# Constant products in TensorE's waits, the last two squares singly, and stages that begin with high-part products

## The reference, cut to what matters

```python
def reference(x, c, ...):                      # x: (1, 256, 1024)
    cond = jax.nn.silu(c)
    for i in range(4):
        mod = (cond @ ada_w[i] + ada_b[i])[:, None, :]
        sh1, sc1, gt1, sh2, sc2, gt2 = jnp.split(mod, 6, axis=-1)
        h = rms_norm(x, norm1_w[i]) * (1 + sc1) + sh1
        y = mixer_of_layer_i(h)                # Mamba-2, RWKV-7, attention, Mamba-2
        x = x + (1 + gt1) * y
        h = rms_norm(x, norm2_w[i]) * (1 + sc2) + sh2
        x = x + (1 + gt2) * swiglu_ffn(h, ffn_w1[i], ffn_w3[i], ffn_w2[i])
    return x

def rms_norm(x, w, eps=1e-6):
    return x * lax.rsqrt(jnp.mean(x * x, axis=-1, keepdims=True) + eps) * w

def swiglu_ffn(h, w1, w3, w2):                 # 1024 -> 2816 -> 1024
    return (jax.nn.silu(h @ w1) * (h @ w3)) @ w2
```

## Time and profile before

| | us |
|---|---|
| median of 3 runs | 1813.46 (1809.7 to 1821.83) |
| the profiled execution | 1818.18 |
| its span, first to last instruction | 1816.1 |
| PE busy | 1697.3 |
| DVE busy | 1314.9 |
| ACT busy | 886.5 |

### The profile page before, as it was taken

The page is one execution under the profiler, slowest core; times in us unless marked ns, Lnnn a source line. Parts: engine busy times, 40 slices in busy tenths (PEclk is TensorE's granted clock), DMA queues, the critical chain, the costliest instruction groups (busy, mean ns, idle before and its releaser), DMA issues.

```text
span 1816.1 us, 37554 instructions
## 1 busy us (share of the span) xinstructions
PE 1697.3 (93%) x15995; PEld 1592.3 (88%) x15995; DVE 1314.9 (72%) x1890; ACT 886.5 (49%) x1242; POOL 20.5 (1%) x62
## 2 busy tenths in 40 slices
PE   4999889999989987799999998899999999999998
PEld 4998788999967876589999887899999998989998
DVE  7897896899573866568996447588967977857553
ACT  3665754544324141344444556444545758645442
POOL 4000000000000000000000000000000000000000
PEclk9999999999989999899999999899999999999999
DMA  9563565999714400049998351399973532448652
GB/s 337 152 194 126 171 217 167 334 351 351 251 47 139 131 4 4 3 141 325 346 340 286 93 162 48 101 324 333 356 282 116 186 117 71 172 143 287 187 187 70
DMA packets 217799, 347.39 MB, mean 191 GB/s; under 512 B 8416, under 2 KB 175024, under 8 KB 217632
## 3 DMA queue, kind: packets, MB, share of 16 engines
q1 hardware_dynamic: 215856, 344.22, 56.1%
q10 hardware_dynamic: 1648, 0.43, 0.1%
q0 software_dynamic: 128, 0.33, 0.1%
HBM read 343.91 MB, written 1.05 MB: 190 GB/s over the span
## 4 chain that ended last, share of the span: by engine, by line
PE 77%; DVE 9%; DMA 5%; ACT 5%; issue 4%; ACTq 0%; DVEq 0%
PE psum_dve L442 27%; PE psum_act L442 26%; PE psum_acc L442 22%; DMA ring<-in_ffn_w_dram 4%; DVE w_lo L1261 2%; DVE arena L1232 2%; ACT w_hi L1782 1%; PE psum_act L445 1%; PE psum_dve L445 1%; DMA arena<-in_ada_b_dram 1%; DVE arena L1400 0%; DVE arena L1438 0%; DVE x L1356 0%; DVE arena L1457 0%; DVE hT L1334 0%
## 5 line engine op out<-in xcount | busy, mean ns | idle before, releaser
L1261 DVE TENSOR_TENSOR w_lo<-ring,w_hi 128x1024 fp32r<-128x1024 f32 x432 | 518.8, 1222 | 193.0 <-ACT w_hi L1782 190.2
L1782 ACT ACTIVATE w_hi<-ring 128x1024 fp32r<-128x1024 f32 x432 | 458.3, 1061 | 395.9 <-DMA ring<-in_ffn_w_dram 232.8
L442 PE MATMUL psum_dve<-h_lo,w_hi 128*128 128x256 f32 x1216 | 341.6, 281 | 0.0
L442 PE MATMUL psum_act<-h_lo,w_hi 128*128 128x256 f32 x960 | 273.1, 284 | 0.0
L1232 DVE SCALAR_TENSOR_TENSOR arena<-ring,vcol,arena 128x512 f32<-128x512 f32 x336 | 239.0, 748 | 5.0 <-DMA ring<-in_ada_w_dram 1.5
L442 PEld LDWEIGHTS psum_dve<-h_lo,w_hi 128*128 128x128 f32 x1216 | 230.0, 189 | 0.0
L442 PE MATMUL psum_act<-h_hi_ffn,w_hi 128*128 128x256 f32 x704 | 201.7, 287 | 11.1 <-DVE h_lo L1331 11.1
L442 PE MATMUL psum_acc<-g_hi,w_hi 128*128 128x256 f32 x704 | 201.1, 286 | 0.0
L442 PE MATMUL psum_act<-h_hi_ffn,w_lo 128*128 128x256 f32 x704 | 201.0, 286 | 0.0
L442 PE MATMUL psum_dve<-h_hi_ffn,w_hi 128*128 128x256 f32 x704 | 197.3, 280 | 0.2 <-DVE w_lo L1261 0.2
L442 PE MATMUL psum_acc<-g_hi,w_lo 128*128 128x256 f32 x704 | 197.4, 280 | 0.0
(11 more groups left out here) (314 smaller groups left out, 3338.6 us busy)
## 6 DMA issues: line engine op xcount, KB each, us to landing
ring<-in_ffn_w_dram SPq DMA_DIRECT2D x132, 1024.0 KB, 7.1
ring<-in_ada_w_dram SPq DMA_DIRECT2D x96, 1024.0 KB, 7.0
ring<-in_m_in_w_dram SPq DMA_DIRECT2D x48, 1024.0 KB, 5.4
ring<-in_m_out_w_dram SPq DMA_DIRECT2D x16, 1024.0 KB, 4.8
ring<-in_r_w_rkv_dram SPq DMA_DIRECT2D x12, 1024.0 KB, 5.4
ring<-in_f_qkvf_w_dram SPq DMA_DIRECT2D x12, 1024.0 KB, 5.3
ring<-in_r_out_w_dram SPq DMA_DIRECT2D x4, 1024.0 KB, 4.8
ring<-in_f_out_w_dram SPq DMA_DIRECT2D x4, 1024.0 KB, 4.8
```

The lines of the kernel that those rows point to most:

```text
L442: return nc.tensor.matmul(o, l, r, start=start, stop=stop, skip_group_check=True)
L1261: tell(V.tensor_tensor(o, raw, hi, ALU.subtract), split_ready, hold=False)
L1782: tell(A(o, raw, ACT.Copy), hi_ready)
```

## The change

- `keep_busy(n)` is new: n plain f32 products of the identity with a constant mask, into `psum_acc[0]`. 20 stand at the start, behind the masks and before the wait for the vectors; 3 before and 4 behind `reduce_part(0, 1)`; one before the last pair of sums of each later norm; behind the sums (and `reduce_part`, where it is) 5 in second norms, 8 in layer 1's first norm, 2 in the first norms of layers 2 and 3.
- The last two tiles are squared singly; a new semaphore tells that the seventh tile is updated.
- `first_tiles` makes the high-part products of all eight tiles first, waiting for `h_hi` alone, and the low-part ones behind them. In a network a third unit's high-part products stand between; its low-part ones and the fourth unit follow.
- DVE scales all eight tiles before the first low part.
- At the start one unit is split before the second modulation part and one behind it, not three before both; the first modulation part is read earlier; ACT splits the two units behind Ln and Exp.

```diff
-FIRST_UNITS = 3
...
+        cond_ready, seventh_ready = sem("cond_ready"), sem("seventh_tile_updated")
...
+            def keep_busy(n):
+                for _ in range(n):
+                    mm(psum_acc[0][:, 0:S], ident[:, :], upto[:, 0:S])
             def freed(key, who):
...
-            def first_tiles(who, narrow=False):
+            def h_high(k):
+                need = KD * (count["split norms"] - 1) + k + 1
+                pe.wait_ge(h_hi_ready, need)
+                return h_hi2[count["which"]][:, k, :]
+            def first_tiles(who, narrow=False, more=None):
+                bn = None
                 if narrow and who == "act":
...
                 else:
-                    bn = open_bank("act") if narrow else None
-                    b = open_bank(who)
+                    if narrow:
+                        bn = open_bank("act")
+                    b, b2 = open_bank(who), open_bank(more) if more else None
                 w = [[v.rearrange("p (k c) -> p k c", k=KD) for v in next_unit()] for u in range(2)]
                 for k in range(KD):
-                    h = h_parts(k)
+                    h = h_high(k)
                     if narrow:
-                        last = mm3(bn[0:M_H, 0:S], (wn_hi[:, k, :], wn_lo[:, k, :]), h, k == 0, k == KD - 1)
+                        mm(bn[0:M_H, 0:S], wn_hi[:, k, :], h, k == 0, False)
+                        mm(bn[0:M_H, 0:S], wn_lo[:, k, :], h, False, False)
+                    for u in range(2):
+                        o = b[:, u * S:(u + 1) * S]
+                        mm(o, w[u][0][:, k, :], h, k == 0 and u == 0, False)
+                        mm(o, w[u][1][:, k, :], h, False, False)
+                if more:
+                    w.append([v.rearrange("p (k c) -> p k c", k=KD) for v in next_unit()])
+                    for k in range(KD):
+                        mm(b2[:, 0:S], w[2][0][:, k, :], h_high(k), k == 0, False)
+                        mm(b2[:, 0:S], w[2][1][:, k, :], h_high(k), False, False)
+                for k in range(KD):
+                    low = h_parts(k)[1]
+                    if narrow:
+                        last = mm(bn[0:M_H, 0:S], wn_hi[:, k, :], low, False, k == KD - 1)
                         if k == KD - 1:
...
                     for u in range(2):
-                        last = mm3(b[:, u * S:(u + 1) * S], (w[u][0][:, k, :], w[u][1][:, k, :]), h, k == 0 and u == 0, k == KD - 1)
+                        last = mm(b[:, u * S:(u + 1) * S], w[u][0][:, k, :], low, False, k == KD - 1)
                         if k == KD - 1 and u == 0:
...
                 bank_read(who)
+                if more:
+                    for k in range(KD):
+                        last = mm(b2[:, 0:S], w[2][0][:, k, :], h_parts(k)[1], False, k == KD - 1)
+                    unit_read(last)
+                    w = [v.rearrange("p (k c) -> p k c", k=KD) for v in next_unit()]
+                    for k in range(KD):
+                        last = mm3(b2[:, S:2 * S], (w[0][:, k, :], w[1][:, k, :]), h_parts(k), k == 0, k == KD - 1)
+                    close_bank(more, last)
+                    bank_read(more)
...
                         bank.append(open_bank("act"))
-                    pe.wait_ge(nsq_ready, 4 * norms[0] + j + 1)
+                    if j == 3 and count["down"]:
+                        pe.wait_ge(acc_free, 4 * count["down"] - 3)
+                        keep_busy(1)
                     for k in (2 * j, 2 * j + 1):
+                        pe.wait_ge(nsq_ready, 5 * norms[0] + (j + 1 if j < 3 else k - 2))
                         last = mm(bank[0][:, 0:S], ones[:, :], nsq[:, k, :], k == 0, k == KD - 1)
...
                         reduce_part(l, 2)
+                    if count["down"]:
+                        keep_busy(5 if which else 8 if l == 1 else 2)
                     norms[0] += 1
...
                 for i in range(KF // 2):
-                    two_tiles("act") if i else first_tiles("act")
-                    two_tiles("dve")
+                    if i == 0:
+                        first_tiles("act", more="dve")
+                    else:
+                        two_tiles("act")
+                        two_tiles("dve")
                 reduced = dict(ffn_reduced(l))
...
             close_bank("act", tr(b[:, 0:KD], vrow[0:KD, 0, :], KD))
+            pe.wait_ge(masks_ready, 1)
+            keep_busy(20)
             pe.wait_ge(vec_landed, 16 * n_vec_dmas)
...
                 first_norm(j)
+            keep_busy(3)
             reduce_part(0, 1)
+            keep_busy(4)
             for l in range(DEPTH):
...
                                                 op0=ALU.mult, op1=ALU.mult), t_ready, hold=False)
-                    if splits and k:
-                        low(k - 1)
                 if splits:
-                    low(KD - 1)
+                    for k in range(KD):
+                        low(k)
                     split_norms[0] += 1
...
                         tell(V.scalar_tensor_tensor(out=x[:, k, :], in0=psum_acc[j][:, u * S:(u + 1) * S], scalar=gate[:, g, k:k + 1],
-                                                    in1=x[:, k, :], op0=ALU.mult, op1=ALU.add), acc_free if u else dve_step, hold=False)
+                                                    in1=x[:, k, :], op0=ALU.mult, op1=ALU.add),
+                             acc_free if u else seventh_ready if j == 3 else dve_step, hold=False)
                 res[0] += 1
...
                     split_narrow(1, M_H)
-            stream(FIRST_UNITS)
-            dve.wait_ge(vcol_ready, 1)
-            reduced_part(0, 0, False)
+                if i == 6:
+                    dve.wait_ge(vcol_ready, 1)
+                    reduced_part(0, 0, False)
+            stream(1)
             reduced_part(0, 1, False)
+            stream(2)
             for l in range(DEPTH):
...
             def norm(l, which):
-                for j in range(4):
+                for j in range(3):
                     if norms[0]:
...
                     tell(A(flat(nsq[:, 2 * j:2 * j + 2, :]), flat(x[:, 2 * j:2 * j + 2, :]), ACT.Square), nsq_ready, hold=False)
-                if (l, which) == (0, 0):
-                    stream(FIRST_UNITS)
+                if norms[0]:
+                    act.wait_ge(seventh_ready, norms[0])
+                tell(A(nsq[:, 6, :], x[:, 6, :], ACT.Square), nsq_ready, hold=False)
+                if norms[0]:
+                    act.wait_ge(acc_free, 4 * norms[0])
+                tell(A(nsq[:, 7, :], x[:, 7, :], ACT.Square), nsq_ready, hold=False)
                 b = take()
...
                 tell(A(rstd[:, :], rstd[:, :], ACT.Exp, scale=-0.5), rstd_ready)
+                if (l, which) == (0, 0):
+                    stream(2)
                 act.wait_ge(mod_ready[which], l + 1)
```

More of the change, by code:

```diff
@@ L239, in trunk @@
         c_landed, qkw_landed, d_landed, dskip_ready = sem("c_landed"), sem("qk_norm_landed"), sem("d_skip_landed"), sem("d_skip_ready")
-        cond_ready = sem("cond_ready")
+        cond_ready, seventh_ready = sem("cond_ready"), sem("seventh_tile_updated")
         mod_ready = [sem(f"mod_ready{i}") for i in range(2)]
```

## The result

Measured side by side, the changed kernel takes 1791.53 us (median of 4, 1784.56 to 1794.24) against 1813.05 us (median of 4, 1809.7 to 1821.83): ratio 0.9872, interval 0.985 to 0.9894. Three more comparisons gave 0.9873, 0.9849 and 0.9882. The gain is 21.5 us, 13.5 were forecast, and the time lies 1 us outside the range.

The account below looks back on a forecast made before the run. PE was taken as the bound, busy 1697.3 of 1816.1 us, leaving 119 us idle and half-clock time to win. Start, norm gains and cap summed to 13.5 us: 1813.46 - 13.5 = 1800, range 1792.5 to 1807.

Parts of the forecast that it names:

- the forecast's own part of it: Whole kernel: the forecast's own range, 1796 to 1806.7 us, given a chance of 0.63.
- Second norms: Second norms of layers 0 to 3: earlier start plus held clock gain 2.0, 3.2, 2.9, 2.0 us before the weights' cap.
- the cap: Networks of layers 1 and 2: PE runs into its weights, limiting second-norm gains from 3.2 to 2.1 and 2.9 to 1.4.
- the earlier start, 0.5: Second norms: after five constants the first real product starts at 308.43, not 308.96, 0.5 us sooner.
- First norms: First norms of layers 1, 2, 3: constants around reduce_part gain 2.4, 1.2, 1.2 us through earlier start and held clock.
- the high bound of 1.75: First norms of layers 2 and 3: upper end of each gain, taken as 1.2 between 0.25 and 1.75 us.
- Start, 1.2: Kernel start: 20 constants and those around reduce_part gain 1.2 us, between 0.3 (clock half through transposes) and 4.3.
- the fall that I feared: Start: the constants' clock is gone before the ones sums, start worth 0.3, total 12.6; one chance in two.
- Layer 2's lead of 0.15 us: Layer 2's network: low half ends at 1259.40, PE uses it at 1259.54; with 1.25 us from earlier transfers, caps gain at 1.4.
- Constants do not hold the clock: Rival, chance 0.12: clock falls as before, only earlier starts remain, 2.8 us gained, 1811 us.
- constants in the way: Rival, chance 0.05: constants at half clock, 0.82 us each, delay each stage's first product; slower, 1826 us.
- No cap, no fall: Rival, chance 0.20: warm start, clock holds through reduce_part, earlier transfers feed layers 1 and 2 in full; about 1793 us.

Follow-up runs that it names:

- the changed one moved back: Changed kernel, its 20 start constants made 42 products of 120 columns, 128 records in all, so the solve lies as in the kernel before: 1795.65 us, ratio 0.9901.
- the kernel before moved: Kernel before plus 42 one-column products in PE's first long wait, moving later work by 84 records: 1807.96 us, ratio 0.9973.
- the order alone: Changed kernel with keep_busy looping no times, so no constants; squares, product order and start order stay: 1808.09 us, ratio 0.9981 to the kernel before.
- the lean start: Changed kernel without the 20 constants at the start and the 3 ahead of reduce_part: 1793.63 us, ratio 0.9888 to the kernel before.
- the tuned kernel: Changed kernel with 14 start constants, modulation parts later in the ring, 2 constants each in head loop and normalisation: 1784.26 us, ratio 0.983 to the kernel before.

## Why the prediction fell short, point by point

**The step that failed** is the sum's silent one: it has terms for eight norms, and takes each stage between them as it was. In its place the runs showed this: every edit that adds instructions to PE moves all later work against the blocks of its code, and in this kernel one stage feels that, by waits for blocks and by the half clock that comes with them. It is 10.2 us in the profiles shown, 6 to 10 over the profiles at the two places (158.8 and 162.1 in the kernel before, 158.8 in the changed one moved back; 151.6 to 152.3 in four profiles of the change, 152.5 in the kernel before moved). Without the solve's 10.2 us the profiled pair differs by 15.0, which is inside the range. Moved back, the change measures 1795.65, inside the range and 0.35 us below the forecast's own part of it. The trace of before had the evidence: waits ended by "issue" add to 23 us on PE there, and I left them unread because they were no part of the change. How a late block turns into a clock that falls in one kernel and holds in the next stays open.

**Second norms, 2.0 each before the cap.** Measured 2.6, 3.9, 3.7, 2.7 against 2.0, 3.2, 2.9, 2.0: right in pattern, each 0.6 to 0.8 short. The term that was mis-sized is the earlier start, 0.5. Counted from the start of the stage (289.0 and 288.3), the sums end at 16.6 instead of 17.2, and the first product starts at 18.9 instead of 20.0: 1.1 earlier. I had priced the five constants at 0.515 each; they take 2.32 us, 0.46 each, since back to back their records overlap, and the sums behind one constant overlap with it too. The saving of 0.44 us per us of half clock held: 3.4 us of it make 1.5, and with the 1.1 that is layer 0's 2.6.

**First norms**, 2.4, 1.2, 1.2: measured 3.1, 1.8, 2.1. The clock holds through reduce_part in layers 2 and 3, so the high bound of 1.75 was nearer. The reason given, the constants, is not shown for layer 2: neither kernel without them there lost the clock behind that norm. In layer 3 it held with the order alone and fell in the kernel without constants behind the first norms. In layer 1 it still falls once, at 541 us, for 3.4 us.

**Start, 1.2**: measured 0.7, 0.9 and 0.8, and 5.3 in one profile. The constants ended at 18.9, not 20.5 us, which left PE idle for longer than reckoned, and the fall that I feared came:

```profile
7.86 11.08 PE L441 MATMUL psum_acc<-upto,ident 128*128 128x256 f32 x40 [5.02 <-POOL small L2229]
21.41 0.44 PE L444 MATMUL psum_act<-ident,arena 128*128 128x128 f32 x2 [2.47 <-DMA arena<-in_ada_b_dram]
22.10 1.53 PE L444 MATMUL psum_act<-ident,arena 128*128 128x128 f32 x4 [0.25 <-ACT vcol L2176]
...
30.73 6.39 PE L441 MATMUL psum_act<-arena,ones 128*128 128x256 f32 x16
```

The clock rose under the constants at about 12 us, PE idled 2.47 us for the vectors, the clock fell at 22.5 while transposes ran, and the sums took 6.39 us at half. The first product came at 43.13, inside the 39 to 43.6 named. By the rule of the Trainium skill, "TensorE: Matmul & The Clock Gate", Part 4, that transposes don't count as products do, this was to be expected, and these rows agree; but the lean start has full clock at 27.6 us behind nothing but transposes, and there they do not.

**The cap, 1.1 and 1.5 taken off**: it is real, and larger. The networks of layers 0, 1 and 2 gave back 1.4, 1.5 and 3.3 us (in the second profile layer 2's network gained 1.2 instead). I had left layer 0 whole. Layer 2's lead of 0.15 us was misread: PE had stood idle for 0.17 us until that low half was done, so there was no lead, and the term should have been 1.25 instead of 1.4. The rest of what layer 2 gave back was a wait. The weights came late: ACT's copy of part_rows stood behind a late w_hi, and PE behind that, with half clock after:

```profile
1285.34 2.15 ACT L1831 ACTIVATE w_hi<-ring 128x1024 fp32r<-128x1024 f32 x2 [0.44 <-DMA ring<-in_ffn_w_dram]
...
1287.51 0.38 ACT L1890 ACTIVATE part_rows<-psum_act 128x256 f32<-128x256 f32 x1
...
1287.95 0.44 PE L444 MATMUL psum_dve<-ident,part_rows 128*128 128x128 f32 x2 [2.03 <-ACT part_rows L1890]
```

So on the terms it named, the forecast said 13.5 us, and the profile has 19.9 + 0.7 - 5.5 (with 0.7 won in the last network) = 15.1.

**The rivals.** "Constants do not hold the clock" and "constants in the way" are out: no 0.50 behind the four second norms. "No cap, no fall" named 1793, near the result, for the wrong reason: both the cap and the fall at the start are there. Its number was met, within 2 us, by a stage that no case spoke of, and that is luck.

## What to carry to other kernels

Before you sum up a change, sort the bound engine's idle time by what ended it, and take waits that no semaphore ended as a cost that any added or removed instruction can move: a kernel has to be compared with itself at another offset (some idle-time products more) before a few tenths of a per cent are put down to an idea. Constants behind a norm's sums held the clock here in all four second norms and cost nothing where they fit in the wait, while behind layer 2's first norm the new order held it without them, so try each group by itself; judge "fits" by the record time at the clock that stands, not by columns. When the product that follows gets earlier, look at the transfer behind it: here 6.2 of the 19.9 us won at the norms went back in the networks, and with the extra loads moved the tuned kernel's three networks take no longer than in the kernel before (163.3 us each and the 0.5 moved out, against 162.7, 164.4 and 165.2).

## What the runs showed of the hardware

- PE's instructions arrive in blocks of 16.4 KB, one per 127.33 matmul records. In the dense work outside the solve no wait falls on the blocks' numbers in any of the 18 executions profiled. The two waits ended by "issue" that stand there (1.82 and 1.14 us in the changed kernel, at records 4013 and 10675) are of another kind: before the change they come at 3929 and 10573, so they move with the work, and their cause is open. In the solve there are 11 to 16 block waits of 0.5 to 2.9 us, some 12 to 18 us in all, in each of the 18. 75 us in the solve of the kernel before, when no weights are loaded at all, have these two queues and nothing else:

```profile
DMA packets 20, 0.31 MB, mean 4 GB/s; under 512 B 0, under 2 KB 0, under 8 KB 0
## 3 DMA queue, kind: packets, MB, share of 16 engines
q8 instruction: 18, 0.29, 1.6%
q14 instruction: 2, 0.02, 0.1%
```

  So it is not the weights' traffic that makes the blocks late in these 75 us. The Trainium skill, "Runtime: NRT & Kernel Launch", section "Instruction fetch mechanics", gives blocks of 16 KiB or 256 instructions, fetched by the sequencer itself, at a cost that is mostly hidden. The trace agrees with the block (127.33 records, each a weight load and a matmul, are 254.7 instructions). It agrees with the hiding in the dense work, where a block lasts 15 us, and not in the solve.
- The clock column reads 1.00 from the first instant until the clock first changes, though the engine starts at half. In 4 us from 8 us on the changed kernel has 10 records of 256 columns, in the next 4 us 20, both with 1.00 in the column:

```profile
8.00:12.00 4.00, 4.00 (x10) 3.19 (x11) 3.86 (x9) 1.07 (x1) 3.30 (x11) 1.00 1.03 369
12.00:16.00 4.00, 4.00 (x20) 3.47 (x19) 3.93 (x7) 0.21 (x1) 3.42 (x10) 1.00 1.04 382
```

  At the start, only the spacing of records tells the clock. The kernel with 126 records of 80 columns stayed at half for 27 us under them.
- In layer 3's network 100 us hold 854 records in the changed kernel and 845 in the earlier trace rows, both with PE busy throughout at 1.00. The tuned kernel has 845 again. Where that per cent comes from is open.

```profile
1620.00:1720.00 100.00, 100.00 (x854) 100.00 (x853) 59.48 (x62) 51.72 (x57) 0.00 (x0) 1.00 0.68 217
```
